# Rotary key copies moved from DVE to ACT, ACT's list reordered at the second layer's input projection, and one wait for all eight keys

## What is computed

```python
def mla_mixer(h, positions, w_in, q_norm, w_uq, kv_norm, w_ukv, w_out):
    B, T, _ = h.shape
    c_q, c_kv, k_rope = split_cols(h @ w_in, ODD_SPLITS)              # 384, 256, 64 columns
    q = (rmsnorm(c_q, q_norm) @ w_uq).reshape(B, T, MLA_HEADS, MLA_NOPE + MLA_ROPE)
    kv = (rmsnorm(c_kv, kv_norm) @ w_ukv).reshape(B, T, MLA_HEADS, MLA_NOPE + MLA_V)
    ...
    q_rope = rope(q_rope, cos[:, :, None, :], sin[:, :, None, :])
    k_rope = rope(k_rope, cos, sin)                                    # one rotary key for all 8 heads
    return chunk_causal_attention(q_nope, q_rope, k_nope, k_rope, v) @ w_out

def reference(...):
    for l in range(DEPTH):
        h = rmsnorm(x, norm_gains[l, 0])
        ...                                                            # m = mixer of the layer
        x = x + rmsnorm(m, norm_gains[l, 1])
        h = rmsnorm(x, norm_gains[l, 2])
        x = x + rmsnorm(sq_relu_mlp(h, mlp_w1[l], mlp_w2[l]), norm_gains[l, 3])
```

## Time and profile before

| | |
|---|---|
| median of three runs | 1199.6 us |
| the profiled execution, its own time | 1199.8 us |
| its span in the profile | 1198.1 us |
| PE busy | 1166.8 us, 97% |
| DVE, ACT, POOL busy | 808.8, 624.6, 120.2 us |
| granted TensorE clock, mean | 0.999 of full speed |
| chain that ended last | PE 83%, DVE 8%, ACT 6%, issue 2%, DMA 1% |

### The profile page before, as it was taken

One profiled execution on the slowest core, in us unless ns is written; L12 is line 12 of the kernel. 1 busy time (PEld: TensorE's weight loads), 2 busy tenths in 40 slices (PEclk: granted clock), 3 DMA queues, 4 the chain that ended last, 5 costly groups with the idle time before them and its releaser, 6 DMA issues.

```text
span 1198.1 us, 16327 instructions
## 1 busy us (share of the span) xinstructions
PE 1166.8 (97%) x5851; PEld 963.2 (80%) x5851; DVE 808.8 (68%) x1232; ACT 624.6 (52%) x1161; POOL 120.2 (10%) x129
## 2 busy tenths in 40 slices
PE   6999999999999999999999999999999999999997
PEld 5777788887888888888888877777978888888886
DVE  4466867885666687678477367864577687668474
ACT  5553655554656355545445766554555544545431
POOL 2222311310021112120000000100000000000000
PEclk9999999999999999999999999999999999999999
DMA  4331122124413332332232232202423232231221
GB/s 129 105 87 54 54 59 66 53 89 141 164 58 104 123 105 88 105 123 71 71 106 85 66 91 60 73 34 88 158 81 105 96 123 87 88 122 53 88 88 70
DMA packets 87490, 108.18 MB, mean 90 GB/s; under 512 B 9186, under 2 KB 48195, under 8 KB 87428
## 3 DMA queue, kind: packets, MB, share of 16 engines
q1 hardware_dynamic: 85684, 101.85, 27.1%
q0 software_dynamic: 1744, 5.51, 1.4%
HBM read 104.20 MB, written 2.10 MB: 89 GB/s over the span
## 4 chain that ended last, share of the span: by engine, by line
PE 83%; DVE 8%; ACT 6%; issue 2%; DMA 1%; POOL 0%; DVEq 0%; SPq 0%; ACTq 0%
PE bank L1856 22%; PE bank L1858 22%; PE bank L1857 22%; PE pp L1857 2%; PE pp L1858 2%; PE pp L1856 2%; PE po L2336 2%; PE pp L1998 1%; PE pp L1901 1%; DVE w_lo L610 1%; ACT w_hi L601 1%; PE pp L2317 1%; ACT w_hi L599 1%; PE po L2009 0%; PE misc L1858 0%
## 5 line engine op out<-in xcount | busy, mean ns | idle before, releaser
L1856 PE MATMUL bank<-h_lo,w_hi 128*128 128x512 f32 (+4 forms) x764 | 292.9, 383 | 8.6 <-DVE h_lo L1321 4.1
L1858 PE MATMUL bank<-h_hi,w_hi 128*128 128x512 f32 (+4 forms) x764 | 289.9, 379 | 0.0
L1857 PE MATMUL bank<-h_hi,w_lo 128*128 128x512 f32 (+4 forms) x764 | 289.7, 379 | 0.0
L1856 PEld LDWEIGHTS bank<-h_lo,w_hi 128*128 128x128 f32 (+1 forms) x764 | 142.5, 187 | 39.1 <-issue 5.1
L1858 PEld LDWEIGHTS bank<-h_hi,w_hi 128*128 128x128 f32 (+1 forms) x764 | 142.5, 186 | 27.2
L1857 PEld LDWEIGHTS bank<-h_hi,w_lo 128*128 128x128 f32 (+1 forms) x764 | 142.6, 187 | 25.7
L1856 PE MATMUL bank<-wx,a_hl 128*128 128x512 f32 x320 | 125.4, 392 | 0.1
L599 ACT CAST wx<-raw 128x1024 fp32r<-128x1024 f32 x72 | 74.6, 1049 | 96.1 <-DVE raw L1551 64.9
L1858 PE MATMUL bank<-wx,a_hl 128*128 128x512 f32 x320 | 124.6, 389 | 0.0
L1857 PE MATMUL bank<-wx,a_hl 128*128 128x512 f32 x320 | 124.5, 389 | 0.0
L1562 DVE TENSOR_TENSOR y<-y,bank 128x512 f32<-128x512 f32 x80 | 54.7, 684 | 87.4 <-PE bank L1858 87.3
(11 more groups left out here) (364 smaller groups left out, 2166.8 us busy)
## 6 DMA issues: line engine op xcount, KB each, us to landing
stage<-in_mlp_w SPq DMA_DIRECT2D x66, 512.0 KB, 3.7
raw<-in_mlp_w SPq DMA_DIRECT2D x50, 512.0 KB, 3.5
stage<-in_ev_w_in SPq DMA_DIRECT2D x28, 512.0 KB, 3.8
spare<-in_mlp_w SPq DMA_DIRECT2D x12, 512.0 KB, 4.6
stage<-in_ev_w_out SPq DMA_DIRECT2D x8, 512.0 KB, 3.5
stage<-in_od_w_out SPq DMA_DIRECT2D x8, 512.0 KB, 3.5
stage<-in_od_w_in SPq DMA_DIRECT2D x10, 256.0 KB, 2.9
x_tok<-in_x SPq DMA_DIRECT2D x4, 512.0 KB, 5.4
```

The source lines that it names most:

```text
L1856: nc.tensor.matmul(dst, wh, xl_, start=first, stop=False)
L1857: nc.tensor.matmul(dst, wl, xh, start=False, stop=False)
L1858: return nc.tensor.matmul(dst, wh, xh, start=False, stop=last)
```

## The change

It has four parts.

1. ACT's order. In the last steps of MLP 0, `token_high(1, 3)` and the split of ("ob", 0) now stand ahead of `x_square` of the last block, inside the loop, and the wait for `x_new` goes; behind `mean_square` and the four small operations stands the split of ("ob", 1). The two ob splits no longer stand behind oa tiles 0 and 1.
2. The four scaled copies of the rotary key move from DVE (`key_rope`, removed) to ACT, behind the copy of line 1228. Each increments `side_ready`, which so counts five for a tile, and takes over from `rope_copied` as the semaphore that frees the bank and releases `turn_q`.
3. PE waits once, at step j = 0 of the attention, for all eight keys, in place of a wait for key h at the first step of each head h.
4. `first_done`, one counter for both output projections, becomes two.

```diff
-        first_done, rope_copied = sem("first_done"), sem("rope_copied")
+        first_done = {j: sem(f"first_done{j}") for j in (0, 2)}
...
-            says(("ob", t), rope_copied, t + 1)
+            says(("ob", t), side_ready, 5 * t + 5)
...
-                        act.wait_ge(first_done, j + t - 1)
+                        act.wait_ge(first_done[j], t - 1)
...
-                    elif KD + NT <= m < 2 * KD - 1 and layer == 0:
+                    elif m >= KD + NT and layer == 0:
                         token_high(j, m - KD - NT)
+                        if m == 2 * KD - 1:
+                            split_high(act, NEXT + m + AHEAD - 2 * KD)
                         x_square(NT * j, m - KD - NT)
 
             mlp(0)
 
 
-            act.wait_ge(x_new[1], KD)
-            x_square(NT, NT - 1)
             mean_square(2 * NT)
...
             nc.scalar.activation(r_in, r_in, ACT.Exp, scale=-0.5).then_inc(eps_ready, 1)
-            token_high(1, NT - 1)
+            split_high(act, unit_no[("ob", 1)])
             act.wait_ge(eps_ready, 4)
...
-                if t < 2:
-                    split_high(act, unit_no[("ob", t)])
-                else:
+                if t >= 2:
                     kv_hi(t - 2)
...
                 nc.scalar.activation(lat[:, t, C_Q + 2 * P:C_KR], b[:, 0:P], ACT.Copy).then_inc(side_ready, 1)
+                dup = lat[:, t, C_KR:C_KR + 2 * P].rearrange("p (s d x c) -> p s d x c", s=2, d=2, x=2)
+                for s, x_ in ((0, 0), (0, 1), (1, 0), (1, 1)):
+                    c0 = P + (x_ if s == 0 else 1 - x_) * RH
+                    one = b[:, c0:c0 + RH].rearrange("p (a c) -> p a c", a=1).to_broadcast([P, 2, RH])
+                    ins = nc.scalar.activation(dup[:, s, :, x_, :], one, ACT.Copy, scale=r_in[:, c])
+                    ins.then_inc(side_ready, 1)
...
-            def key_rope(t):
-                dve.wait_ge(side_ready, t + 1)
...
-                    ins = nc.vector.tensor_scalar(dup[:, s, :, x_, :], one, r_in[:, t:t + 1], None, ALU.mult)
-                ins.then_inc(rope_copied, 1)
...
-                pe.wait_ge(rope_copied, t + 1)
+                pe.wait_ge(side_ready, 5 * t + 5)
...
-                    pe.wait_ge(kt_ready, h + 1)
+                if j == 0:
+                    pe.wait_ge(kt_ready, MLA_HEADS)
```

More of the change, by code:

```diff
@@ L1733, in _ @@
             split_low(dve, unit_no[("mv", 0)])
-            key_rope(0)
             kv_lo(2)
             split_low(dve, unit_no[("mv", 0)] + 1)
-            key_rope(1)
             kv_lo(3)
             split_low(dve, unit_no[("mv", 0)] + 2)
-            key_rope(2)
             q_lo(0)
             split_low(dve, unit_no[("mv", 0)] + 3)
-            key_rope(3)
             for t in range(1, NT):
@@ L1933, in out_head @@
                 if idx == KD - 1:
-                    ins.then_inc(tile_done if t < 2 else first_done, 1)
+                    ins.then_inc(tile_done if t < 2 else first_done[j], 1)
             EO_ORDER, OO_ORDER = HEAD, list(range(KD))
```

## The result

The changed kernel takes 1207.5 us, the median of four executions (1206.2 to 1208.7), against 1199.6 (1199.2 to 1199.8) before: a ratio of 1.0065, 95% interval [1.005, 1.008]. That is +7.9 us, slower, the way that was forecast, but above the range of 1203.0 to 1206.8. The experiments compare with more executions of the kernel before; over all 65 of them its mean is 1200.3 us, so 0.7 us of the 7.9 come from the four executions behind the 1199.6, which were faster than usual.

A forecast was written before the change was run, and what follows sets the result against it. The prediction took PE's own list of matmuls to bound the kernel, busy 1166.8 of 1198.1 us. Its terms, 3.0 + 0.8 + 1.3 = 5.1 us on 1199.6, gave 1204.7 us, range 1203.0 to 1206.8.

The forecast's parts named there:

- Term 1: Before oa tile 2, PE stops because ACT has 4.8 us of work ahead of oa tile 0's eviction: +3.0 us.
- Term 2: At the second mv tile, PE waits for ACT's list, lengthened by the key copies: +0.8 us.
- R: Time that four key copies take from ACT's list for each ob tile: 0.8 us, between 0.45 and 1.2.
- Term 3: At the first scores, PE waits for all eight keys, so the projection behind starts later: +1.3 us.
- Nothing gives it back: Behind 735 us, PE's 10.4 us of idle time is short waits that recover none of the 5.1 us.
- The sum: Over the three changed places, 3.0 + 0.8 + 1.3 = 5.1 us added.
- The range: Whole kernel: 1203.0 (both uncertain terms low) to 1206.8 us (dear copies, other terms' upper ends), without clock or give-back.
- The clock falls: Rival: PE's 2.9 us stop amid the oa tiles drops the clock to 1.2 GHz, giving 1210 us; chance 0.04.
- The price of 5.4 us: At the oa tiles, one tile run wholly at 1.2 GHz would take 5.4 us longer.

The follow-up runs named there:

- The kernel before, again: The kernel before run again with no edit: 1201.2 us, ratio 1.0005 [0.9994, 1.0016].
- the repeats: The unchanged kernel before, run again: 1201.2 us; the changed kernel, run again three times without an edit: 1207.1, 1206.3 and 1207.2 us.

## Why the prediction was wrong

- **Term 1**, the stop at oa tile 2: +3.0 forecast, 2.78 measured. Right, by its own steps: ACT's list in front of the eviction took 4.83 us for 4.8 (668.82 to 673.65), and PE reacted in 0.06 us, not 0.15. One split less gives half of the stop, and without the splits it is gone.
- **Term 2**, the copies: +0.8 forecast, 0.75 measured, R = 0.78 for 0.8. The estimate from the Trainium skill's page "ScalarE: Activation LUTs", section "What ACT_TABLE_LOAD costs" (0.96 for four), was too high here: a single copy lasted 0.31 to 0.33 us, near the 0.33 of that estimate, but they started 0.20 us apart and not 0.24.
- **Term 3**, the keys: +1.3 forecast, 1.29 measured, with the idle time of 2.33 us before scores 0 and none before the projection.
- **"Nothing gives it back"**: 0.5 us did, nearly all of it near 830 us, a small error. The sum was 5.1 us and the stops came to 4.3.
- **The baseline**: 0.7 us of the miss is that the kernel before has a mean of 1200.3 us, not 1199.6. Its own layer-0 stop and the late weight load make both kernels scatter by several us, which no row of one profile shows.
- **The range**: its upper end, 1206.8, is 0.2 more than its own terms give (3.1 + 2.4 + 1.5 = 7.0, or 1206.6). It changes nothing.

**The step that failed** is the reason against the rival "The clock falls", and with it the chance of 0.04 and the zero for the clock in the sum and the range. It was that PE once stood idle for 2.58 us and the granted clock was 1.00 over those 3 us. The printed 1.00 is not what the array ran at. Behind that stop, matmuls of 128x256 start 0.21 us apart; the same form starts 0.12 us apart behind the next stop, at 27 us:

```profile
15.34 0.41 PE L1857 MATMUL bank<-h_hi,w_lo 128*16 128x256 f32 x1
15.55 0.41 PE L1858 MATMUL bank<-h_hi,w_hi 128*16 128x256 f32 x1
...
27.14 0.28 PE L1857 MATMUL bank<-h_hi,w_lo 128*16 128x256 f32 x1
27.26 0.28 PE L1858 MATMUL bank<-h_hi,w_hi 128*16 128x256 f32 x1
```

So the array was at the lower level behind the very stop that was to show that it stays up; whether it had been up ahead of it, the row can't tell. The kernel before, again, has the same stop (2.57 us): its matmuls start 0.12 us apart behind it, and from 16.6 us on 0.21, with a granted clock of 0.57 over 16 to 20 us:

```profile
15.36 0.28 PE L1857 MATMUL bank<-h_hi,w_lo 128*16 128x256 f32 x1
...
16.79 0.41 PE L1856 MATMUL bank<-h_lo,w_hi 128*16 128x256 f32 x1
...
16.00:20.00 4.00, 4.00 (x23) 3.00 (x22) 3.17 (x5) 0.83 (x4) 0.00 (x0) 0.57 0.72 207
```

In 6 of the 14 profiles the matmuls right behind this stop are at the fast pace, and in all six they drop to the slow one within 1.5 us; in the other eight they are slow at once. Read by its pace, the row says nothing against the rival, and the repeats speak for it. What the runs showed in place of the zero: behind stops of this length in the changed places the clock fell 8 times in 13, at 1.4 to 1.6 us a fall. The rule cited, that an idle array falls back to the lower level (Trainium skill, "TensorE: Matmul & The Clock Gate", Part 1), pointed the right way. The price of 5.4 us was too high in turn.

**The stop at the scores** was never weighed for the clock, though by the prediction's own sum PE would stand still there for over 2 us (from 728.43 - 0.36 = 728.07 to 730.4). In half of the four profiles of the changed kernel that was the place.

With one fall in each execution the forecast would have been 1206.2, inside the range, so the clock is the step that failed but not the whole miss: 0.7 us are the baseline, and 1.3 of the 7.1 us between the means stay unexplained. What also stays open is why the stop of 1.90 us near 140 us is there in some executions and 0.16 in others, and what decides which of two equal stops loses the clock; whether ACT's list or the semaphores take part in it was not tried.

## What to carry to other kernels

Where PE is the bound, count the stops that an edit makes on PE by their length as well as their sum: here no stop of 0.9 to 1.6 us was followed by a clock fall, those of 1.9 us in layer 0 were in 8 of 11 profiles, and those of 2.3 to 2.6 us in 8 of 13 cases, at 1.4 to 1.6 us each. Ask it of every stop in the changed schedule. A list on another engine has room only up to the moment its next result is wanted: here 2.06 us, and 4.8 were put in. When a printed clock is to carry an argument, check it against the distance between starts of matmuls of one form. And before a difference of half a per cent is split into terms, know how far the same kernel scatters.

## What was not expected of the hardware

- The granted clock fell behind stops of 1.9 to 2.6 us (0.66 and 0.76 as the mean of stretches of 5 and 7 us), and not every time behind equal stops.
- In the first 20 us a stretch can print a granted clock of 1.00 while the matmuls run at half pace (0.21 us apart for 256 columns, against 0.12 later).
- A stop of 4.76 us cost no more clock in the stretch behind it than one of 2.61 (0.66 in both).
- The same kernel ranged from 1196.9 to 1204.2 us on one chip. Its profiles differ by such falls, by a stop in layer 0 of 0.16 or 1.90 us, and by a weight load that lands over 1 us later in some executions.
